# Another PSUM bank for the second half of the next group's rows, in the expert stage of a two-block layer

## The chip, the cores and the metric

The kernel runs on one core of one Trainium2 chip. The time is that of the device in microseconds, as the median of the timed runs. The engines are TensorE (PE, matmuls and transposes), VectorE (DVE), ScalarE (ACT), GpSimd (POOL, here gathers and scatters) and SyncE (SP, here loads). PE writes only to PSUM, of which there are eight banks of 128 x 512 words, ps0 to ps7.

## The reference

Two blocks of a model follow each other on 2048 tokens of width 1024, in float32. The first is a mixer of five parts, the second attention and a mixture of experts. The change is in the last: each token chooses 4 of 32 experts, and each expert is applied to the tokens that chose it.

```python
def _clamped_swiglu(hgu):
    x_glu = jnp.minimum(hgu[..., ::2], SWIGLU_LIMIT)
    x_lin = jnp.clip(hgu[..., 1::2], -SWIGLU_LIMIT, SWIGLU_LIMIT)
    return x_glu * jax.nn.sigmoid(SWIGLU_ALPHA * x_glu) * (x_lin + 1.0)

    # in _moe_sequence
    xs = h[tok]
    hgu = lax.ragged_dot(xs, w_gate_up, group_sizes) + b_gate_up[e_sorted]
    act = _clamped_swiglu(hgu)
    out = lax.ragged_dot(act, w_down, group_sizes) + b_down[e_sorted]
    out = out * gates.reshape(-1)[order][:, None]
    return jax.ops.segment_sum(out, tok, num_segments=L)
```

## The kernel before

Seven stages follow each other, each ended by a meeting of all engines. The sixth, `experts_stage` with `experts_sync`, `experts_pool`, `experts_pe`, `experts_act` and `experts_dve`, is the one with the change; it lies between some 3080 and 5950 us.

**The work.** The tokens of an expert stand in blocks of 128. Up to four blocks of one expert make a group; with these inputs there are 32 groups of one to four blocks, 78 blocks in all. Every engine runs the same loop over the groups (`groups`). `r` is the number of blocks of this group, `rn` that of the next; both are read from a table that an earlier stage made, so block b is done only if `r > b` (`present`). A group has six steps, c = 0 to 5. In c = 0 to 3 the rows of a block (width 1024) are multiplied by a quarter of the gate and up weights, 512 columns, and DVE and ACT gate the product to 256 activations. In c = 4 and 5 the 1024 activations are multiplied by a half of the down weights.

**The precision.** A float32 value is split into a high part (rounded, cast by ACT) and a low part (what is left, subtracted by DVE, `low`). A product of 128 x 1024 by 1024 x 512 is 8 turns over k of three matmuls each: high by high, high by low, low by high, 24 in all (L2407). The weights are split as they arrive: ACT casts a step's weights in four pieces (`high`), DVE subtracts in four (`lows`), both one step ahead of PE, in block 0 of each step.

**The transposes.** PE needs rows and activations transposed. There are two kinds, and they stand between the turns of a product (`between` says in which):

- `acts(c, b)`: 2 transposes (L2390) of block b's 256 new activations. In step c = 4 those of step 3 come at k = 0 of block b's product.
- `rows(b, hf, t)`: 4 transposes (L2383) of one half of block b's rows of the **next** group, gathered by POOL into `e_hx`. The half hf = 0 comes at k = 2 and hf = 1 at k = 6 of block b's product in c = 4, if `rn > b`. Blocks that the next group has and this one lacks come together at k = 6 of c = 5 (`bulk`).

Either kind goes to one of three PSUM banks, `E.T[0..2]`, which are ps5, ps6 and ps7. PE takes the bank's semaphore `t_free`, transposes into it and raises `t_full`. ACT casts the high part out of the bank and raises `t_hi`. DVE subtracts the low part out of the bank and raises `t_free` (in `low(...).then_inc(E.t_free[t], 1)`). `take` waits for a semaphore and counts it down (L2244); the waiting instruction holds up everything behind it on its engine. `acts` uses bank b % 2. `rows` uses what `rows_bank(b, hf, bulk)` names, and PE, ACT and DVE all call it with the same arguments. Its line 2255, `b % 2 if hf else 2` for rows that are not in bulk, is the one that the change touches.

**The order around the change.** It is written out by hand. In c = 4 PE does for each block b: acts(3, b), k = 0 and 1, rows(b, 0), k = 2 to 5, rows(b, 1), k = 6 and 7, and then acts(3, b+1) of the next block. DVE does in block 0: its part of acts(3, 0), a weight piece, rows(0, 0), two weight pieces, rows(0, 1), a weight piece, and then `outcome(4, 0)` when PE has finished the product; in later blocks the same without the weights.

Of the kernel before, what the change touches and what calls it, by code (L numbers as in the profile page):

```python
# [2250 lines left out]

def rows_bank(b, hf, bulk):


    return (2 * b + hf) % 3 if bulk else b % 2 if hf else 2


def present(eng, r, b):
# [17 lines left out]
def between(eng, c, b, r, rn, acts, rows, k):  # L2276

    if k == (0 if c == 4 else 2 if b else 4) and 1 <= c <= 4:
        acts(c - 1, b)
    if k in (2, 6) and c == 4:  # L2280
        with eng.If(rn > b):
            rows(b, k // 4, rows_bank(b, k // 4, False))
    if k == 6 and c == 5 and b == 0:
        for j in range(1, 4):
            with eng.If(r <= j):
                with eng.If(rn > j):
                    rows(j, 0, rows_bank(j, 0, True))
                    rows(j, 1, rows_bank(j, 1, True))
# [601 lines left out]
```

## Time and profile before

| | us |
|---|---|
| median of the timed runs (3) | 6026.62 |
| lowest and highest | 6026.35, 6033.98 |
| the profiled execution, its own time | 6033.98 |
| its span in the profile | 6032.8 |
| PE busy | 5627.3 (93%) |
| DVE busy | 3616.4 (60%) |
| ACT busy | 2339.7 (39%) |
| POOL busy | 815.5 (14%) |

The profile is of one execution. Its page lists the busy time of each engine, the costliest groups of instructions, and what ended their idle time. "PEq L2244" as what ended a wait means that PE's sequencer stood in a `take`; PEld is the loading of PE's weights, which overlaps its matmuls. A timeline row has the start, the duration, the engine, the line, the operation with its output and inputs (bank numbers left out, so ps5 and ps6 both read ps), the count, and in brackets the idle time before it. The end of a matmul is modelled and reaches past the next one's start: the distance from start to start is its pace. The profiled execution took 7.4 us more than the median; what a part of the change costs is worked out from its rows and holds for both.

### The profile page before, as it was taken

The page shows a single profiled execution, that of the slowest core. Times are in us where ns is not written, and L with a number is a line of the kernel's source. Part 1 is how long each engine was busy: PE and PEld are TensorE (multiplying, and loading weights), DVE is VectorE, ACT ScalarE, POOL GpSimd, SP SyncE. Part 2 cuts the span into 40 slices and gives each one's busy share as a digit, 9 for nine tenths or more (in the row PEclk, how much of TensorE's full clock was granted, in tenths as well). Part 3 has the DMA queues.
Part 4 walks back from the last instruction along what each step waited for, and adds up shares of the span by engine and source line. Part 5 has one row for each costly group of instructions (what it writes and reads, how often), then busy time and mean ns, then how long its engine had stood idle before and what let it go on. Part 6 is the DMA issues. An engine that isn't in the chain of part 4 may idle for free. (4 is left out here: it accounts for less than half of the span.)

```text
span 6032.8 us, 81187 instructions
## 1 busy us (share of the span) xinstructions
PE 5627.3 (93%) x26367; PEld 4475.4 (74%) x26368; DVE 3616.4 (60%) x6999; ACT 2339.7 (39%) x4594; POOL 815.5 (14%) x612
## 2 busy tenths in 40 slices
PE   8999988987999999996979999999999999998994
PEld 7877766876777777765758788888887787876783
DVE  6666666322555566665755655655666645566667
ACT  3444412333333344442423433433445434344443
POOL 1110134322000000002520001000100000000102
PEclk9999999998999999998989999999999999999997
DMA  4333153445111101004324545544656535466666
GB/s 141 115 109 112 67 169 127 114 114 158 64 50 48 43 22 43 23 8 149 136 105 168 178 147 181 189 156 158 216 187 233 209 119 178 134 232 237 235 230 204
DMA packets 247513, 830.79 MB, mean 138 GB/s; under 512 B 20880, under 2 KB 153600, under 8 KB 206080
## 3 DMA queue, kind: packets, MB, share of 16 engines
q1 hardware_dynamic: 217152, 737.13, 34.5%
q0 software_dynamic: 27680, 85.41, 5.9%
q10 hardware_dynamic: 2336, 4.45, 0.2%
q8 instruction: 119, 1.95, 0.1%
q14 instruction: 226, 1.85, 0.1%
HBM read 689.78 MB, written 137.13 MB: 137 GB/s over the span
## 5 line engine op out<-in xcount | busy, mean ns | idle before, releaser
L2407 PE MATMUL ps<-e_wh,e_hTh 128*128 128x512 f32 x2496 | 1014.1, 406 | 14.0 <-PEq L2244 14.0
L2509 DVE TENSOR_TENSOR e_wl<-r_raw,e_wh 128x1024 fp32r<-128x1024 f32 x772 | 907.9, 1220 | 183.7 <-DVEq L2244 179.1
L2407 PE MATMUL ps<-e_wl,e_hTh 128*128 128x512 f32 x2496 | 992.6, 398 | 0.0
L2407 PE MATMUL ps<-e_wh,e_hTl 128*128 128x512 f32 x2496 | 991.9, 397 | 0.0
L2448 ACT CAST e_wh<-r_raw 128x1024 fp32r<-128x1024 f32 x772 | 769.4, 1049 | 21.2 <-ACTq L2244 16.1
L2407 PEld LDWEIGHTS ps<-e_wh,e_hTh 128*128 128x128 f32 x2496 | 472.4, 189 | 123.0 <-issue 19.4
L2407 PEld LDWEIGHTS ps<-e_wh,e_hTl 128*128 128x128 f32 x2496 | 472.3, 189 | 115.0
L2485 ACT ACTIVATE e_gg<-e_gg 128x256 f32<-128x256 f32 x312 | 130.4, 418 | 1101.2 <-ACTq L2244 1101.2
L2407 PEld LDWEIGHTS ps<-e_wl,e_hTh 128*128 128x128 f32 x2496 | 473.4, 190 | 103.1
L1652 PE MATMUL ps<-a_PT,a_V 128*128 128x512 f32 (+1 forms) x1088 | 548.9, 596 | 0.7 <-ACT a_oT L1708 0.7
L1721 DVE TENSOR_REDUCE a_sc<-ps 128x1 f32<-128x416 f32 (+1 forms) x640 | 364.7, 587 | 262.2 <-PE ps L1630 262.2
L2407 PE MATMUL ps<-e_wh,e_aTh 128*128 128x512 f32 x1248 | 515.0, 413 | 0.5 <-PEq L2244 0.5
L2407 PE MATMUL ps<-e_wl,e_aTh 128*128 128x512 f32 x1248 | 495.7, 397 | 0.0
L2407 PE MATMUL ps<-e_wh,e_aTl 128*128 128x512 f32 x1248 | 495.5, 397 | 0.0
L1630 PE MATMUL ps<-a_K,a_Q 128*128 128x416 f32 (+1 forms) x1920 | 455.5, 367 | 27.5 <-DMA a_KR<-kTd 24.4
L1630 PEld LDWEIGHTS ps<-a_K,a_Q 128*128 128x128 f32 x1920 | 356.0, 189 | 83.8 <-issue 77.1
L2540 DVE TENSOR_TENSOR e_tt<-ps,e_bg 128x512 f32<-128x512 f32 x312 | 215.2, 690 | 292.9 <-DVEq L2244 290.8
L1638 PEld LDWEIGHTS ps<-ident,a_P 128*128 128x128 f32 (+1 forms) x2176 | 258.6, 138 | 170.4 <-issue 131.2
L1701 ACT ACTIVATE a_P<-ps,a_sc 128x416 f32<-128x416 f32 (+1 forms) x640 | 377.5, 605 | 0.1
L385 PE MATMUL ps<-m_xh,m_wh 128*128 128x512 f32 x896 | 353.8, 395 | 5.3 <-DVE m_wl L670 5.3
L1735 DVE COPY a_PT<-ps 128x512 f32<-128x512 f32 x384 | 265.1, 691 | 152.0 <-PE ps L1638 152.0
L385 PE MATMUL ps<-m_xh,m_wl 128*128 128x512 f32 x896 | 349.7, 390 | 0.0
(353 smaller groups left out, 9247.8 us busy)
## 6 DMA issues: line engine op xcount, KB each, us to landing
r_raw<-in_wgu SPq DMA_DIRECT2D x130, 2048.0 KB, 7.8
r_raw<-in_wdn SPq DMA_DIRECT2D x64, 2048.0 KB, 8.1
m_raw<-in_w SPq DMA_DIRECT2D x56, 1024.0 KB, 4.9
e_bg<-in_bgu SPq DMA_DIRECT2D x32, 1024.0 KB
qTd<-p_qt SPq DMA_DIRECT2D x32, 640.0 KB, 6.6
e_bd<-in_bdn SPq DMA_DIRECT2D x32, 512.0 KB, 11.0
kTd<-p_kt SPq DMA_DIRECT2D x32, 448.0 KB, 3.7
a_Q<-qTd SPq DMA_DIRECT2D x7, 2048.0 KB, 8.0
```

What stands on the lines that cost most here:

```text
L385: t = pe.matmul(p[:, :], x[:, w, i, j * 128:(j + 1) * 128], y[:, c % 2, i, :], start=(n == 0), stop=(n == 23))
L1630: t = pe.matmul(p[:, 0:w], x, y, start=(n == 0), stop=(n == len(todo) - 1))
L1638: t = pe.transpose(p[0:n, k * 128:(k + 1) * 128], P.P[:, m % 2, c * 512 + k * 128:c * 512 + k * 128 + n], ident[:])
L1652: t = pe.matmul(ps[b][:, :], P.V[0:r, n % 2, j, :], P.PT[0:r, G % 2, j, :], start=(j == 0), stop=(j == NT - 1))
L1701: act.activation(P.P[:, m % 2, lo:lo + w], p[:, 0:w], ACT.Exp, bias=P.sc[:, m % 2, 6:7], scale=scale, accum_out=P.sc[:, m % 2, 8 + c:9 + c ...
L1721: dve.tensor_reduce(z[:, c:c + 1], p[:, 0:SCW[c][1]], AX, ALU.max).then_inc(*v.step("max", m, c))
L1735: dve.tensor_copy(P.PT[:, G % 2, 4 * c:4 * c + 4, q], p[:, :].rearrange("p (k q) -> p k q", k=4)).then_inc(*v.step("t", n, c))
L2407: t = pe.matmul(E.G[g][:, :], x[:, b, k, :], y[:, c % 2, k, :], start=(n == 0), stop=(n == 23))
L2448: act.copy(E.wh[:, n % 2, 2 * i:2 * i + 2, :].rearrange("p k n -> p (k n)"), E.raw[:, n % 2, 2 * i:2 * i + 2, :].rearrange("p k n -> p (k ...
L2485: act.activation(E.gg[:], E.gg[:], ACT.Silu, scale=SWIGLU_ALPHA).then_inc(E.sig, 1)
L2509: return dve.tensor_tensor(lo, src, hi.bitcast(F32), ALU.subtract)
L2540: link(dve.tensor_tensor(E.tt[:], E.G[g][:, :], E.bg[:, c * 512:(c + 1) * 512], ALU.add))
```

## The change

For a row half of kind hf = 1 that is not in bulk, the bank becomes (b + 1) % 2 in place of b % 2. On all three engines that use it, the same instructions stand in the same order; the bank that they name and the semaphore that they take or raise are the other one. Since a blank line went as well, every line below it is one less in the changed kernel (L2383 becomes L2382).

```diff
 def rows_bank(b, hf, bulk):
 
-
-    return (2 * b + hf) % 3 if bulk else b % 2 if hf else 2
+    return (2 * b + hf) % 3 if bulk else (b + 1) % 2 if hf else 2
```

The first place is on PE, step c = 4, the end of block 0 and the start of block 1. In brackets are the semaphores that an instruction takes; `e_t_free0` goes with ps5 and `e_t_free1` with ps6. Before:

```order
L2383 MATMUL ps5<-ident,e_hx 128x128 [waits e_t_free0]
L2383 MATMUL ps5<-ident,e_hx 128x128 x3
L2281 UNCONDITIONAL_BRANCH
L2407 MATMUL ps0<-e_wh,e_aTh 128x512 [waits e_aT_full0]
L2407 MATMUL ps0<-e_wl,e_aTh 128x512
L2407 MATMUL ps0<-e_wh,e_aTl 128x512
L2407 MATMUL ps0<-e_wh,e_aTh 128x512
L2407 MATMUL ps0<-e_wl,e_aTh 128x512
L2407 MATMUL ps0<-e_wh,e_aTl 128x512
L2260 COMPARE_AND_BRANCH
L2390 MATMUL ps6<-ident,e_act 128x128 [waits e_g_free1,e_aT_full1,e_act_full1,e_t_free1]
L2390 MATMUL ps6<-ident,e_act 128x128
```

Now:

```order
L2382 MATMUL ps6<-ident,e_hx 128x128 [waits e_t_free1]
L2382 MATMUL ps6<-ident,e_hx 128x128 x3
L2280 UNCONDITIONAL_BRANCH
L2406 MATMUL ps0<-e_wh,e_aTh 128x512 [waits e_aT_full0]
L2406 MATMUL ps0<-e_wl,e_aTh 128x512
L2406 MATMUL ps0<-e_wh,e_aTl 128x512
L2406 MATMUL ps0<-e_wh,e_aTh 128x512
L2406 MATMUL ps0<-e_wl,e_aTh 128x512
L2406 MATMUL ps0<-e_wh,e_aTl 128x512
L2259 COMPARE_AND_BRANCH
L2389 MATMUL ps6<-ident,e_act 128x128 [waits e_g_free1,e_aT_full1,e_act_full1,e_t_free1]
L2389 MATMUL ps6<-ident,e_act 128x128
```

Nothing moved. The rows' transposes (from e_hx) name ps6 and take `e_t_free1` instead of ps5 and `e_t_free0`, and the activations' transposes of block 1 (from e_act) name ps6 and take `e_t_free1` as they did: the same bank, six matmuls later.

The second place is on DVE, the same passage, from two weight pieces of block 0 to the low part of block 1's activations. Before:

```order
L2509 TENSOR_TENSOR e_wl<-r_raw,e_wh 128x1024 [waits e_hi_full] x2
L2281 COMPARE_AND_BRANCH
L2509 TENSOR_TENSOR e_hTl<-ps5,e_hTh 128x512 [waits e_t_hi0]
L2506 MEMSET e_junk 1x1 x2
L2281 UNCONDITIONAL_BRANCH
L2509 TENSOR_TENSOR e_wl<-r_raw,e_wh 128x1024 [waits e_hi_full]
L2506 MEMSET e_junk 1x1
L2552 SCALAR_TENSOR_TENSOR e_Y<-ps0,e_bd 128x512 [waits e_g_full0,e_out_free0]
L2506 MEMSET e_junk 1x1
L2260 COMPARE_AND_BRANCH
L2509 TENSOR_TENSOR e_aTl<-ps6,e_aTh 128x256 [waits e_t_hi1]
```

Now:

```order
L2508 TENSOR_TENSOR e_wl<-r_raw,e_wh 128x1024 [waits e_hi_full] x2
L2280 COMPARE_AND_BRANCH
L2508 TENSOR_TENSOR e_hTl<-ps6,e_hTh 128x512 [waits e_t_hi1]
L2505 MEMSET e_junk 1x1 x2
L2280 UNCONDITIONAL_BRANCH
L2508 TENSOR_TENSOR e_wl<-r_raw,e_wh 128x1024 [waits e_hi_full]
L2505 MEMSET e_junk 1x1
L2551 SCALAR_TENSOR_TENSOR e_Y<-ps0,e_bd 128x512 [waits e_g_full0,e_out_free0]
L2505 MEMSET e_junk 1x1
L2259 COMPARE_AND_BRANCH
L2508 TENSOR_TENSOR e_aTl<-ps6,e_aTh 128x256 [waits e_t_hi1]
```

Here too only the bank and the semaphore of the e_hTl subtraction are others. In block 1 it is the other way round: its rows went to ps6 and now go to ps5, which is the bank of acts(3, 2).

## Rows read from the trace of the kernel before

**Rows 1.** The page: the span, and section 1 (busy us, share, instructions).
```profile
span 6032.8 us, 81187 instructions
...
PE 5627.3 (93%) x26367; PEld 4475.4 (74%) x26368; DVE 3616.4 (60%) x6999; ACT 2339.7 (39%) x4594; POOL 815.5 (14%) x612
```

**Rows 2.** Busy time by stretch, the experts' stage (length, then PE, PEld, DVE, ACT, POOL).
```profile
3107.00:5947.00 2840.00, 2784.03 (x12447) 2236.39 (x12445) 1736.09 (x3347) 1190.37 (x1759) 262.89 (x215) 0.99 0.55 187
```

**Rows 3.** Waits 3107:5947, PE's own: who, for whom, us, times, longest.
```profile
PE ps L2390 <- PEq L2244: 36.7, 15, 5.1
...
PE ps L2407 <- PEq L2244: 13.5, 10, 3.5
...
PE ps L2383 <- PEq L2244: 5.3, 3, 1.9
```

**Rows 4.** Timeline of PE, 3204.8:3208.4, block 0 to 1 (start us, duration us, ...).
```profile
3204.87 0.60 PE L2383 MATMUL ps<-ident,e_hx 128*128 128x128 f32 x4
...
3206.47 0.40 PE L2407 MATMUL ps<-e_wh,e_aTl 128*128 128x512 f32 x1
3206.71 0.38 PE L2390 MATMUL ps<-ident,e_act 128*128 128x128 f32 x2
```

**Rows 5.** Timeline of ACT, 3203.2:3210.9, the cast of the rows.
```profile
3205.59 0.59 ACT L2439 CAST e_hTh<-ps 128x512 fp32r<-128x512 f32 x1
```

**Rows 6.** Timeline of DVE, 3203.2:3211.2, the same passage.
```profile
3205.19 2.35 DVE L2509 TENSOR_TENSOR e_wl<-r_raw,e_wh 128x1024 fp32r<-128x1024 f32 x2
3207.45 0.68 DVE L2509 TENSOR_TENSOR e_hTl<-ps,e_hTh 128x512 fp32r<-128x512 f32 x1
...
3210.51 0.42 DVE L2509 TENSOR_TENSOR e_aTl<-ps,e_aTh 128x256 fp32r<-128x256 f32 x1
```

**Rows 7.** Timeline of all engines, 3715:3717.5, a group of three blocks.
```profile
3715.77 0.38 PE L2390 MATMUL ps<-ident,e_act 128*128 128x128 f32 x2
...
3716.63 0.68 DVE L2509 TENSOR_TENSOR e_hTl<-ps,e_hTh 128x512 fp32r<-128x512 f32 x1
```

**Rows 8.** Timeline of all engines, 5859:5861.3, the last passage, two blocks.
```profile
5859.52 0.38 PE L2390 MATMUL ps<-ident,e_act 128*128 128x128 f32 x2
...
5860.55 0.68 DVE L2509 TENSOR_TENSOR e_hTl<-ps,e_hTh 128x512 fp32r<-128x512 f32 x1
```

**Rows 9.** Timeline of all engines, 3211.4:3213.9, block 1 to 2.
```profile
3211.58 0.60 PE L2383 MATMUL ps<-ident,e_hx 128*128 128x128 f32 x4
...
3212.30 0.59 ACT L2439 CAST e_hTh<-ps 128x512 fp32r<-128x512 f32 x1 [2.66 <-ACTq L2244]
...
3213.03 0.69 DVE L2509 TENSOR_TENSOR e_hTl<-ps,e_hTh 128x512 fp32r<-128x512 f32 x1 [1.26 <-DVEq L2244]
...
3213.41 0.38 PE L2390 MATMUL ps<-ident,e_act 128*128 128x128 f32 x2
```

**Rows 10.** Timeline of all engines, 4649:4651, PE's transposes waiting for DVE.
```profile
4649.65 0.43 DVE L2545 SCALAR_TENSOR_TENSOR e_act<-e_act,e_gg 128x256 f32<-128x256 f32 x1 [0.48 <-DVEq L2244]
...
4650.38 0.41 PE L2390 MATMUL ps<-ident,e_act 128*128 128x128 f32 x2 [0.62 <-PEq L2244]
```

**Rows 11.** Timeline of POOL and PE, 5100:5117, a gather and a wait for it.
```profile
5100.92 1.31 POOL L2326 DMA_INDIRECT e_hx<-h1d,e_idx  x1 [31.63 <-POOLq L2244]
...
5112.14 1.06 PE L2383 MATMUL ps<-ident,e_hx 128*128 128x128 f32 x8 [1.94 <-PEq L2244]
...
5113.35 0.63 PE L2407 MATMUL ps<-e_wl,e_aTh 128*128 128x512 f32 x1
...
5113.78 0.63 PE L2407 MATMUL ps<-e_wh,e_aTl 128*128 128x512 f32 x1
```

**Rows 12.** Timeline of PE, 3384.5:3387, another such wait.
```profile
3385.06 1.13 PE L2383 MATMUL ps<-ident,e_hx 128*128 128x128 f32 x8 [1.62 <-PEq L2244]
...
3386.26 0.39 PE L2407 MATMUL ps<-e_wl,e_aTh 128*128 128x512 f32 x1
3386.50 0.39 PE L2407 MATMUL ps<-e_wh,e_aTl 128*128 128x512 f32 x1
```

## The prediction, made before the changed kernel was run

> **What bounds the kernel now.** The page's busy shares come first: TensorE (PE) is busy for 93% of a span of 6032.8 us [rows 1]. I then cut out the stage in which the edited function acts, the experts: between 3107 and 5947 us PE is busy 2784 of 2840 us, VectorE (DVE) 1736 [rows 2]. The list of waits for the same stretch names PE's idle time in it: 36.7 + 13.5 + 5.3 = 55.5 us, in 15 + 10 + 3 = 28 waits [rows 3]. So the stage ends when PE ends, and a microsecond that PE newly waits in it is a microsecond of the total, unless one of those 28 waits takes it back.
>
> Last come the timelines of one place, the passage from block 0 to block 1 in step c = 4 of a group. The reader is to see four things in them. PE transposes the second half of the next group's rows at 3204.87, has six matmuls left of block 0, and starts the transposes of block 1's activations at 3206.71 [rows 4]: 1.84 us from one to the other. ScalarE (ACT) casts the rows out of PSUM at 3205.59 for 0.59 us [rows 5]. DVE forms their low part only at 3207.45, because two weight subtractions, 2.35 us from 3205.19, stand ahead of it; it ends at 3207.45 + 0.68 = 3208.13 [rows 6]. That end is what frees the bank. Before, no one asks for that bank until far later.
>
> **The change part by part.** It moves no instruction and adds none. In c = 4 it gives the transposed second half of block b's rows the bank (b+1)%2 instead of b%2.
>
> *What it removes.* Before, these rows took the bank that activations (3, b) had used 18 matmuls earlier. The tightest such place is block 1, where DVE is late with the activations: they end at 3210.51 + 0.42 = 3210.93 [rows 6], and PE's row transposes start at 3211.58 [rows 9] with no idle time noted before them. So the removed wait costs nothing today: 0, and at most some 0.1 us at 28 places, 3 us.
>
> *What it adds.* Now the rows of block b lie in the bank that activations (3, b+1) take next, six matmuls later, and PE's take of t_free there has to see DVE's subtraction end. Behind that waiting transpose stands everything of PE, since it runs in order: the 24 matmuls of block b+1 and all that follows. ACT and DVE do not wait for it with work of their own for long; they are behind PE at this point.
>
> How soon PE starts after DVE has released it is read from a wait of the same transposes on DVE: the releasing instruction ends at 4649.65 + 0.43 = 4650.08, and PE starts at 4650.38, 0.30 us later [rows 10]. There PE passes two takes after the release, here one, so 0.30 is the upper end and 0.15 a lower estimate, half of it. I take 0.30. The price of a place is DVE's end + 0.30 - PE's start of today:
>
> - block 0 to 1, first kind: 3208.13 + 0.30 - 3206.71 = 1.72 us [rows 4, 6]; 5 such places (groups of four blocks)
> - block 0 to 1, second kind: 3716.63 + 0.68 + 0.30 - 3715.77 = 1.84 us [rows 7]; 7 places (groups of three)
> - block 0 to 1, third kind: 5860.55 + 0.68 + 0.30 - 5859.52 = 2.01 us [rows 8]; 16 places (groups of two)
> - block 1 to 2 and 2 to 3: here no weight work is ahead of DVE, and the bare chain counts. Transposes at 3211.58, cast 3212.30 to 3212.89, subtraction 3213.03 to 3213.72, PE's start today 3213.41: 3213.72 + 0.30 - 3213.41 = 0.61 us [rows 9]; 14 places
>
> The places are counted along the timeline: a run of four row transposes, six matmuls, two activation transposes. There are 42, the first at 3204.87 [rows 4] and the last the one that ends at 5859.52 [rows 8]. The sum is 5 x 1.72 + 7 x 1.84 + 16 x 2.01 + 14 x 0.61 = 8.6 + 12.9 + 32.2 + 8.5 = **62 us**. With 0.15 for the release it is 42 x 0.15 = 6 less, 56.
>
> *What takes some of it back.* Three of PE's 28 waits stand in groups of two blocks that are followed by a group of four, in c = 5, behind such a place: PE waits for the gathered rows of the fourth block, 5.3 us in all [rows 3]. One of them ends at 5112.14 after 1.94 us, and its gather had been issued at 5100.92 [rows 11], released by DVE's work on block 0's rows, which does not move. PE will come 2.01 us later and find it done, so these 5.3 us vanish. The other 25 waits (50.2 us) stand nearly all in the three groups of a single block, which contain no place of the new kind, and there DVE's work starts from PE's own products, so it moves along: nothing back. Bounds: 0 and 55.5 back; I take 5.3.
>
> *What the clock adds.* The new pauses on PE will be about 1.5 to 1.9 us long (the price less the 0.16 us by which the last matmul's record reaches past the next start). Of pauses near that length the trace has both outcomes. After 1.62 us the next matmuls stand 0.24 us apart (3386.26, 3386.50) [rows 12], the pace of the granted full level of 2.4 GHz. After 1.94 us they stand 0.43 apart (5113.35, 5113.78) [rows 11], the 1.2 GHz level, and there are eight of those: 8 x 0.19 = 1.5 us. The shorter of the new pauses look like the former, the 16 long ones are between the two. Bounds: none, and all 28 first pauses, 43 us. I take five falls, 8 us, as the long pauses are nearer to the upper row, but a fall also depends on where the pause lies.
>
> The Trainium skill (TensorE: Matmul & The Clock Gate, section "HAM oscillation — how this bites in real kernels") says that a kernel which pauses PE long enough in every turn of its loop pays the slow clock again in every turn. The 1.94 us row agrees that one pause can do it; the 1.62 us row says that a similar one need not. By the rule in its full force this edit pays the second rival below.
>
> The sum: 62 - 5 + 8 = 65 us, on the profiled execution's own time of 6033.98 us: 6099. The median of the three timed runs is 6026.62, 7.4 us less, and the new waits are the same in it: 6026.6 + 65 = 6091.6. Since 0.30 us for the release is its upper end, I round down: **6090 us**, slower by 1.05%.
>
> **The rivals.**
>
> 1. *DVE catches up.* The long price of block 0 comes from the weight subtractions ahead of the rows [rows 6]. If PE's pauses let DVE enter c = 4 less late, all 42 places would cost the bare chain of 0.61: 42 x 0.61 = 26 us, less 1.8 at the three gathers: 6027 + 24 = 6051. For: DVE is idle over a third of the stage [rows 2]. Against: its lateness in c = 4 begins with the gating of PE's last product of c = 3, so it is counted from PE's own time and returns in each group.
>
> 2. *The clock falls at every first pause.* 28 x 1.5 = 43 us beside 62 - 5 = 57: 6027 + 100 = 6127. For: the 1.94 us pause [rows 11]. Against: the 1.62 us one [rows 12].
>
> 3. *The price is given back: not slower.* One mechanism: a PE that pauses in c = 4 meets its later waits late, and each of the 28 shrinks by as much as DVE, ACT and the gathers have gone on meanwhile. If all 55.5 us [rows 3] came back, 62 - 55.5 leaves 6.5 us: 6033, within what counts as no change. It decides at the group's edge: DVE would have to carry its lead into the next group. Against: there its first instruction is the outcome of PE's last product, so it starts level again; and the waits are gathered in a few places, while the new ones are spread over 28 groups.
>
> 4. *The change does nothing, or gains.* That needs the bank to be free by the time PE asks. The bare chain is 3213.72 - 3211.58 = 2.14 us against 1.83 us of PE's cover [rows 9], at its very shortest; no place of the 42 has slack. I give it no chance of its own beyond 1 in 50, with 6027 less up to 3 us.
>
> **How the numbers follow.** Forecast 0.68, with a range of its own of 6075 to 6112 (release 0.15 and no fall; fifteen falls more). Rival 1 0.12, rival 2 0.13, rival 3 0.05, rival 4 0.02. A measurement of this kernel can tell about 0.2%, 12 us, from no change. Faster by more than that 0.01, within it 0.06, slower 0.93. The range that should hold the time 8 times in 10 leaves out rivals 1, 3 and 4 (0.19) and takes in rival 2: 6068 to 6130.
>
> **What would show it right or wrong.** In the changed kernel's list of waits PE's activation transposes should wait at 15 + 42 = 57 places instead of 15, for some 36.7 + 55 us (the recorded pause is a little shorter than the price), and the row transposes no longer at three. The first place should read 3208.13 for DVE's end, as before, and about 3208.4 for PE's start instead of 3206.71. Rival 1 would show new waits that are all near 0.5 us; rival 2 a lower granted clock in the stage and matmuls 0.43 us apart after each first pause; rival 3 a smaller wait in the single-block groups. If DVE's subtraction of the rows ended before PE asks, or PE's pause were not followed by a later end of the group by as much, the forecast would be wrong.

## The result and the profile after

| | before | changed |
|---|---|---|
| median, us | 6026.49 (4 runs) | 6079.91 (4 runs) |
| lowest, highest | 6024.47, 6033.98 | 6075.45, 6086.48 |
| the profiled execution, own time | 6033.98 | 6083.43 |
| its span | 6032.8 | 6082.3 |

The ratio of the times is 1.0086, with a 95% interval of 1.0073 to 1.0098: the changed kernel is slower by 53 us of the medians (44 to 59 by the interval). The two profiled executions are 49.5 us apart. The forecast was 6090.

All but 1.3 us of the 49.5 lies in the experts' stage. From the first matmul of its first group to its last, PE took 2840.2 us before (3106.03 to 5946.19) and 2888.3 now (3106.88 to 5995.21): 48.2 us more. Busy time by stretch of the changed kernel, columns as in [rows 2]:

```profile
3107.00:5995.00 2888.00, 2791.88 (x12447) 2234.62 (x12448) 1736.00 (x3349) 1193.02 (x1759) 263.62 (x216) 0.99 0.54 184
```

DVE's work is the same to 0.1 us (1736.00 against 1736.09) and the stage is 48 us longer. PE's waits in it, which answer to [rows 3]:

```profile
PE ps L2389 <- PEq L2244: 81.3, 57, 3.6
...
PE ps L2406 <- PEq L2244: 10.8, 5, 3.5
...
PE ps L2382 <- PEq L2244: 4.9, 3, 1.7
```

The activation transposes wait at 57 places in place of 15: 42 new ones, the number foretold. The first place, PE's timeline 3205.7:3209.9, answers to [rows 4]:

```profile
3205.80 0.60 PE L2382 MATMUL ps<-ident,e_hx 128*128 128x128 f32 x4
...
3207.40 0.40 PE L2406 MATMUL ps<-e_wh,e_aTl 128*128 128x512 f32 x1
3209.21 0.41 PE L2389 MATMUL ps<-ident,e_act 128*128 128x128 f32 x2 [1.42 <-PEq L2244]
...
3209.69 0.40 PE L2406 MATMUL ps<-e_wl,e_aTh 128*128 128x512 f32 x1
```

and DVE's timeline 3206:3212 to [rows 6]:

```profile
3206.12 2.35 DVE L2508 TENSOR_TENSOR e_wl<-r_raw,e_wh 128x1024 fp32r<-128x1024 f32 x2
3208.39 0.68 DVE L2508 TENSOR_TENSOR e_hTl<-ps,e_hTh 128x512 fp32r<-128x512 f32 x1
...
3211.44 0.42 DVE L2508 TENSOR_TENSOR e_aTl<-ps,e_aTh 128x256 fp32r<-128x256 f32 x1
```

The reader is to see that PE asks for the bank at about 3207.6, six matmuls after the rows, and that DVE's subtraction of those rows ends at 3208.39 + 0.68 = 3209.07. PE starts at 3209.21, 0.14 us after it. From the rows' transposes to DVE's end it is 3.27 us, as before (3204.87 to 3208.13, 3.26): DVE is as late as it was, only someone waits for it now. A later passage, all engines, 3214:3216.8, answers to [rows 9]:

```profile
3214.11 0.60 PE L2382 MATMUL ps<-ident,e_hx 128*128 128x128 f32 x4
...
3214.83 0.59 ACT L2438 CAST e_hTh<-ps 128x512 fp32r<-128x512 f32 x1 [2.66 <-ACTq L2244]
...
3215.57 0.69 DVE L2508 TENSOR_TENSOR e_hTl<-ps,e_hTh 128x512 fp32r<-128x512 f32 x1 [2.56 <-DVEq L2244]
...
3216.40 0.41 PE L2389 MATMUL ps<-ident,e_act 128*128 128x128 f32 x2 [0.29 <-PEq L2244]
```

Here the chain is bare: 3214.11 to 3216.40 is 2.29 us, against 1.83 of six matmuls before.

What a group costs more is read from the start of its step c = 0 to that of the next group. For the second last group, of two blocks, these are two starts of PE's timeline of before and two of the changed kernel's:

```profile
5806.67 0.39 PE L2407 MATMUL ps<-e_wh,e_hTh 128*128 128x512 f32 x1
...
5877.43 0.39 PE L2407 MATMUL ps<-e_wh,e_hTh 128*128 128x512 f32 x1
```

```profile
5853.78 0.39 PE L2406 MATMUL ps<-e_wh,e_hTh 128*128 128x512 f32 x1
...
5926.43 0.39 PE L2406 MATMUL ps<-e_wh,e_hTh 128*128 128x512 f32 x1
```

70.76 us against 72.65: 1.89 more. Read so for every group, the steps c = 4 and 5 together grew by 1.88 to 1.93 us in groups of two blocks (one passage), by 2.19 in groups of three (two passages), by 2.08 in the three groups of four whose next group has two blocks (two passages) and by 2.55 in the two whose next group has four or three (three passages). Steps c = 0 to 3 did not grow. The exceptions are told further down.

### The profile page after: what moved, and what is told of

Same layout as the page of the kernel before. It is cut to its first block and busy times, and to the rows that moved or that the text cites. A ratio compares the mean times of both kernels' runs of the same rounds, so it can differ in the third digit from the quotient of the medians.

```text
span 6082.3 us, 81187 instructions
## 1 busy us (share of the span) xinstructions
PE 5637.7 (93%) x26367; PEld 4475.4 (74%) x26368; DVE 3617.8 (59%) x6999; ACT 2340.9 (38%) x4594; POOL 816.9 (13%) x612
## 5 line engine op out<-in xcount | busy, mean ns | idle before, releaser
L385 PE MATMUL ps<-m_xl,m_wh 128*128 128x512 f32 x896 | 350.0, 391 | 0.0
```

The source lines that it names most:

```text
L385: t = pe.matmul(p[:, :], x[:, w, i, j * 128:(j + 1) * 128], y[:, c % 2, i, :], start=(n == 0), stop=(n == 23))
```

## The experiments

Line numbers are those of before in all six. "Per group" is the growth of c = 4 and 5 over before, read as above. Ratios, and the us that follow from them, are to runs of the kernel before made beside the experiment: their median is 6031.3 for the first four experiments and 6036.5 for the last two.

### The new bank for block 0 alone

```diff
-    return (2 * b + hf) % 3 if bulk else b % 2 if hf else 2
+    return (2 * b + hf) % 3 if bulk else ((b + 1) % 2 if b == 0 else b % 2) if hf else 2
```

> The new bank for block 0 alone; blocks 1 to 3 keep their old one. Theory (each passage costs DVE's end + release - PE's start, the release now read as 0.15 us from the changed kernel's rows): the 28 first passages pause, the 14 later ones do not. 5 x 1.58 + 7 x 1.70 + 16 x 1.88 = 50 us, less some 8 us that single-block groups gave back in the changed kernel: +42 us over before, 35 to 52; groups of two longer by 1.89 us, of three by 1.71, of four by 1.6. Rival (the pauses help each other, or the later passages hide part of the first): the time is that of the whole change, +53, or well under +35.

Measured: ratio 1.0062 (1.0047 to 1.0076), so +37 us (28 to 46). Per group 1.89 us in groups of two, 1.72 of three, 1.60 of four. PE's transposes of activations wait at 43 places, 15 + 28:

```profile
PE ps L2390 <- PEq L2244: 84.4, 43, 5.1
```

The theory holds to 0.02 us a passage. The total is at the low side of the forecast, and the interval covers most of it.

### The new bank for blocks 1 to 3 alone

```diff
-    return (2 * b + hf) % 3 if bulk else b % 2 if hf else 2
+    return (2 * b + hf) % 3 if bulk else ((b + 1) % 2 if b > 0 else b % 2) if hf else 2
```

> The new bank for blocks 1 to 3 alone. Theory: only the 14 later passages pause, each by the bare chain: 14 x (2.14 + 0.15 - 1.83 + 0.03) = 14 x 0.48 = +6.8 us, or 0.11%, groups of two unchanged, of three longer by 0.48, of four by 0.97. Rival (the later passages pause only since PE has paused before them in the same group): 0 at all of them.

Measured: ratio 1.0008 (1.0000 to 1.0017), +5 us (0 to 10). The time alone would not settle it; the profile does. Groups of two are unchanged (0.01 us), groups of three grew by 0.48 and of four by 0.95, and there are 15 + 14 waits:

```profile
PE ps L2390 <- PEq L2244: 38.0, 29, 5.1
```

So the later passages pause of themselves, and the two halves of the change add: 1.72 + 0.48 = 2.20 in groups of three, where the whole change has 2.19.

### The new bank, the second half of the rows two turns earlier

```diff
-    return (2 * b + hf) % 3 if bulk else b % 2 if hf else 2
+    return (2 * b + hf) % 3 if bulk else (b + 1) % 2 if hf else 2
...
-    if k in (2, 6) and c == 4:
+    if k in (2, 4) and c == 4:
...
-                        for k in (0, 2, 6):
+                        for k in (0, 2, 4, 6):
```

The last line changes in the loops of ACT and of DVE.

> The changed kernel with the second half of the rows transposed at k = 4 instead of k = 6, so that twelve matmuls instead of six lie before the bank's next use, and DVE has one weight piece instead of two ahead of it. Theory (the distance to the next use is what matters, not which bank): at later passages PE's cover is 1.83 + 1.40 = 3.23 us against a chain of 2.29: no pause. At block 0 DVE ends one piece (1.17 us) earlier: 0.41, 0.53 and 0.71 us are left, 5 x 0.41 + 7 x 0.53 + 16 x 0.71 = 17 us, less up to 8 given back: +9 to +17 over before. Rival (the bank itself, its shared use, costs): still above +40.

Measured: ratio 1.0019 (1.0010 to 1.0028), +11 us (6 to 17). The waits are 43, so the 14 later passages no longer pause:

```profile
PE ps L2390 <- PEq L2244: 51.3, 43, 5.1
```

The timeline of the first group, 3199:3215, shows both kinds. At block 0 a pause of 0.28 is left, since DVE still has a weight piece ahead of the rows; at block 1 the activation transposes at 3210.96 come without one, as DVE was done at 3209.18 + 0.69 = 3209.87:

```profile
3204.23 0.41 PE L2390 MATMUL ps<-ident,e_act 128*128 128x128 f32 x2 [0.28 <-PEq L2244]
...
3209.18 0.69 DVE L2509 TENSOR_TENSOR e_hTl<-ps,e_hTh 128x512 fp32r<-128x512 f32 x1 [0.34 <-DVEq L2244]
...
3210.96 0.38 PE L2390 MATMUL ps<-ident,e_act 128*128 128x128 f32 x2
```

The banks are the changed kernel's, and four fifths of the loss are gone. It is not the bank as such that costs, it is how soon it is asked for again.

### Both halves of the rows in the third bank

```diff
-    return (2 * b + hf) % 3 if bulk else b % 2 if hf else 2
+    return (2 * b + hf) % 3 if bulk else 2
```

> Both halves of the rows in the third bank (ps7), so the second half at k = 6 waits for the first half's subtraction, and the activations' banks are never in question. Theory: the same formula at another place. First half's end on DVE + 0.15 - PE's start of the second half is 0.54 to 0.87 us at 28 of 31 blocks 0 in the trace of before, 20.6 us in all; 0.33 to 0.66 at block 1, 12.9 us in all, but that much smaller by the pause at block 0, as DVE's lateness there does not grow with it: +20 to +27 us. Rival (what hurts is only the six-matmul distance before activations): +0.

Measured: ratio 1.0033 (1.0021 to 1.0044), +20 us (13 to 27). Per group 0.85, 0.69 and 0.56 us in groups of two, three and four. The same subtraction in the trace of before gives 0.83, 0.67 and 0.54 for block 0 alone, within the 0.54 to 0.87 of the expectation: block 1's lateness did hide behind block 0's pause. The new waits are at the row transposes, 28 of them at block 0; the other six are two at each of the three gathers, where before there was one. The activation transposes have their old 15:

```profile
PE ps L2390 <- PEq L2244: 35.2, 15, 5.1
...
PE ps L2383 <- PEq L2244: 20.6, 34, 0.9
```

A bank that neither kernel had disputed was given a short distance, and the same subtraction of three numbers gave its price.

### DVE subtracts block 0's rows one weight piece earlier

```diff
 (with the changed kernel's rows_bank; DVE's lows)
-                between(dve, c, 0, r, rn, acts, rows, 2 * i)
+                for k in ((0,), (2,), (4, 6), ())[i] if c == 4 else (2 * i,):
+                    between(dve, c, 0, r, rn, acts, rows, k)
```

> The changed kernel, but DVE subtracts the second half of block 0's rows after two weight pieces in place of three; PE and ACT as in the changed kernel. Theory (the first passage is dear since weight pieces stand ahead on DVE): one piece, 1.17 us, less at each of 28: 5 x 0.41 + 7 x 0.53 + 16 x 0.71 = 17, and 14 later ones at 0.48 = 7: 24 us, less up to 8 given back: +16 to +24 over before, 29 to 37 below the changed kernel. Rival (DVE's order does not matter, PE would wait for ACT's cast or the transposes): as the changed kernel.

Measured: ratio 1.0035 (1.0022 to 1.0048), +21 us (13 to 29), so some 32 us of the changed kernel's 53 are gone with one move on DVE. There are again 57 waits, but 55.6 us in place of 81.3:

```profile
PE ps L2390 <- PEq L2244: 55.6, 57, 5.1
```

Per group 0.75 in groups of two, 1.06 of three, 1.43 of four. In groups of four what is left at block 0 is the bare chain: 2.30 us from the rows' transposes to the activations', 2.29 at the later passages. In groups of two it is 2.56, 5881.30 to 5883.86 in the second last group. ACT's timeline 5880:5884.6 there:

```profile
5880.38 2.02 ACT L2448 CAST e_wh<-r_raw 128x1024 fp32r<-128x1024 f32 x2
5882.28 0.60 ACT L2439 CAST e_hTh<-ps 128x512 fp32r<-128x512 f32 x1
```

The cast starts 0.98 us behind the transposes, against 0.72 in the bare chain, as two weight casts stand ahead of it, and DVE, which has one weight piece left ahead, starts the subtraction at 5883.03, right behind that piece and 0.15 us behind the cast's end. So the rival, that PE would wait for ACT's cast anyway, falls for the 1.1 us a passage that the move gave back, and may hold for the 0.27 us that groups of two still pay over the bare chain; no run here separates ACT from DVE in that rest.

### DVE subtracts block 0's rows after all four weight pieces

```diff
 (with the changed kernel's rows_bank; DVE's lows)
-                between(dve, c, 0, r, rn, acts, rows, 2 * i)
+                if c != 4 or i < 3:
+                    between(dve, c, 0, r, rn, acts, rows, 2 * i)
...
+        if c == 4:
+            between(dve, c, 0, r, rn, acts, rows, 6)
         over(E.raw_free[n % 2])
```

> The changed kernel, but DVE subtracts the second half of block 0's rows after all four weight pieces. Theory: 1.17 us more at each of the 28 first passages, 33 us above the changed kernel: +86 over before if the clock stays. The pauses are then 2.6 to 2.9 us long, and what is open of the clock shows here: pauses of 1.4 to 1.74 us had no matmul at 0.43 us pace behind them in the changed kernel, 28 times of 28. If these longer ones do have them, 7 or 8 matmuls slower by 0.19 us each come on top, up to 28 x 1.5 = 42 us: +86 to +128, with fewer or more falls.

Measured: ratio 1.0194 (1.0177 to 1.0211), +117 us (107 to 127). The waits grew by 34.6 us over the changed kernel's 81.3, the 28 x 1.17 = 33 foretold:

```profile
PE ps L2390 <- PEq L2244: 115.9, 57, 3.6
```

The rest is the clock. A passage of a group of two, PE's timeline 5905:5912.5:

```profile
5908.81 0.64 PE L2390 MATMUL ps<-ident,e_act 128*128 128x128 f32 x2 [2.83 <-PEq L2244]
5909.09 0.78 PE L2407 MATMUL ps<-e_wh,e_aTh 128*128 128x512 f32 x1
5909.67 0.63 PE L2407 MATMUL ps<-e_wl,e_aTh 128*128 128x512 f32 x1
5910.09 0.63 PE L2407 MATMUL ps<-e_wh,e_aTl 128*128 128x512 f32 x1
...
5911.37 0.63 PE L2407 MATMUL ps<-e_wh,e_aTl 128*128 128x512 f32 x1
```

From the second on, the matmuls behind the pause stand 0.43 us apart, the 1.2 GHz level; in the changed kernel, at the same place, 0.24. This is so at 21 of the 28 long pauses. A group of two without it grew by 3.03 us over before, one with it by 4.59: a fall costs 1.56 us, and 21 x 1.56 = 33. With the changed kernel's 48.2 and the 33 of DVE, the sum is 114, and this stage grew by 115.6.

## Why the prediction was right, point by point

**Which engine bounds, and where the wait is.** Right. The pause is at the bank's next use, at 42 places, and each is paid in full by the group's length.

**The price of a passage.** Its form, DVE's end plus the release minus PE's start of today, held within 0.03 us a passage in the change and in four further kernels, and within 0.06 in the other two. The term that was mis-sized is the release. I took 0.30 us, from a wait behind which PE passes two takes [rows 10], and named 0.15 as the lower end. It is 0.14 (3209.07 to 3209.21). A pause also puts the following matmuls some 0.03 us further off. So the prices are 1.58, 1.70, 1.88 and 0.48 us in place of 1.72, 1.84, 2.01 and 0.61, and the sum is 5 x 1.58 + 7 x 1.70 + 16 x 1.88 + 14 x 0.48 = 57 us, not 62.

**The clock.** Wrong in size: five falls, 8 us, were counted, and there was none. The 28 first pauses of the changed kernel are 1.40 to 1.74 us long and behind none of them is a matmul at the slow pace. Of the two rows that I stood between, the 1.62 us one [rows 12] was the right one to go by. The 1.94 us row did not stand for its length either: the same wait was 1.76 us long in the kernel with the later passages alone, and there the clock stayed up. Its PE timeline, 5121:5124:

```profile
5121.49 1.06 PE L2383 MATMUL ps<-ident,e_hx 128*128 128x128 f32 x8 [1.76 <-PEq L2244]
...
5122.63 0.40 PE L2407 MATMUL ps<-e_wl,e_aTh 128*128 128x512 f32 x1
5122.86 0.39 PE L2407 MATMUL ps<-e_wh,e_aTl 128*128 128x512 f32 x1
```

In the same kernel it also stayed up behind such a wait of 1.86 us, at 4764.31. Rival 2 falls for this change, but it was a matter of a microsecond: at 2.54 to 2.88 us the last experiment has 21 falls of 28, rarely in groups of four (1 of 5, at 2.54) and nearly always in groups of two (14 of 16, at 2.83 to 2.88). The Trainium skill (TensorE: Matmul & The Clock Gate, "HAM oscillation — how this bites in real kernels") has the rule that a loop which pauses PE long enough pays the slow clock again in every turn. That experiment agrees in 21 of its 28 turns; the change, with pauses of up to 1.74 us, paid it in none.

**The three gathers.** The step failed as I put it. Their wait did go, and another took its place. In the changed kernel the gather is issued at 5139.44, and PE's next group's rows start at 5149.56. All engines, 5149:5154:

```profile
5149.56 1.57 PE L2382 MATMUL ps<-ident,e_hx 128*128 128x128 f32 x12
...
5151.86 1.89 DVE L2508 TENSOR_TENSOR e_hTl<-ps,e_hTh 128x512 fp32r<-128x512 f32 x3
...
5152.69 0.63 PE L2382 MATMUL ps<-ident,e_hx 128*128 128x128 f32 x4 [1.57 <-PEq L2244]
```

Before, PE stopped after eight transposes for the gathered fourth block. Now it does twelve and stops before the last four, which need the bank that the first four of this stretch took: DVE's first subtraction ends at 5151.86 + 0.69 = 5152.55, and PE starts 0.14 us later. Waits of 5.3 us became 4.9. I had asked whether the gather would be done, not what stood behind it.

**What came back all the same.** Of the 57 us, 48.2 show between the two profiles. The groups name the rest. Two shrinkages belong, most likely, to the one profiled execution of before and not to the change, since all seven other profiles have them, the one with only the later passages too (1.72 and 2.23 us). One is the fall behind the 1.94 us wait [rows 11], 1.8 us. The other is in c = 0 to 3 of the group that starts at 5585.44, 2.7 us: of its two waits the second was 2.99 us and is 1.70, and 11 matmuls at the slow pace became 5. Further, small waits in c = 0 to 3 and c = 5 near the groups of one block shrank, as PE came later: 0.42 us at each of three groups of two that stand ahead of one, 0.42 and 0.24 at two others, and 0.8 to 1.4 in c = 0 to 3 of each of the three groups of one block, whose c = 4 and 5 changed by -0.2, -0.3 and +1.1. That is some 4 us in all, so rival 3 is true in small. Those at the groups of two recur in all five experiments with pauses at block 0 and not in the one without; those in the groups of one block recur too, by 0.2 to 1.2 us. Which engine's lead they come from I did not test.

I had put nearly all of the 50.2 us of other waits into the three groups of one block. Only 35 us stand there; 14.5 us stand in c = 0 to 3 of the three groups of two right behind them.

**The sum.** 57 for the passages less 4 given back is 53, and the medians are 53 us apart. So close an agreement is partly luck: single waits behind a group of one block differ between profiles by over 2 us (0.83 and 1.50 us before, 3.23 and 3.00 in the kernel with block 0 alone, in the groups that start at 4683.04 and 5455.49 before). The forecast, 63 over before, had 62 - 5 + 8 = 65, rounded down: 5 too much for the release, 8 too much for the clock, and 5 taken back at a place that gave nothing. That about as much came back elsewhere is luck.

**Rival 1**, DVE catches up, falls: DVE's end is 3.27 us behind the rows' transposes, as before, and 3.54 against 3.55 before in the second last group. The experiment with DVE one weight piece earlier shows what less of that lateness is worth: some 32 us. **What was removed** was worth nothing: no group got shorter in c = 4.

## What to carry to other kernels

A buffer's number matters through the distance to its next use. Take from the trace the moment at which its last reader ends, add the release, subtract the moment at which the next writer starts today: if the outcome is positive, and the writer's engine is the one that bounds, it is the price of each such place, and a helper with one line of arithmetic can hold 42 of them. And when a wait is expected to vanish, ask which semaphore of the same stretch is next.

## What the runs showed of the hardware

- From the end of a DVE instruction that releases a bank to PE's next transpose: 0.14 us with one take behind it, 0.30 with two before the same transposes. In the trace behind [rows 10] the records of the two takes, at 4650.12 and 4650.27, lie 0.15 us apart; the first comes 0.04 us after DVE's end.
- TensorE's clock stayed at 2.4 GHz behind 28 pauses of 1.40 to 1.74 us, in the change and again in the kernel with block 0 alone, and fell to 1.2 GHz behind 21 of 28 of 2.54 to 2.88 us. In the trace of before it fell behind one of 1.94 us at a gather, and stayed up behind the same wait of 1.76 us and another of 1.86 us in the kernel with the later passages alone.
- A fall cost 1.56 us in a group of two blocks (4.59 against 3.03 us), on top of the pause of 2.83 us that it followed.
